# Two layers on one core: small loads, latent norms, head splits and sine tables cut up and placed elsewhere

## What is computed

```python
h = rmsnorm(x, norm_mix_g)
proj = h @ w_in                      # c_q 512, c_kv 256, k_rope, dq, dk, dv, iq, ik, iw, then gates 2 x 2048
q = rmsnorm(c_q, q_norm_g) @ w_uq    # 8 heads; latent norm over 512
ckv = rmsnorm(c_kv, kv_norm_g)       # latent norm over 256
k_nope, v = ckv @ w_uk, ckv @ w_uv
o_a = chunk_causal_attention(q, k, v)            # 8 heads of 128
o_b = attention of 8 heads over 64 keys that an index score selects
merged = sigmoid(gate_a) * (o_a @ w_branch_a) + sigmoid(gate_b) * (o_b @ w_branch_b)
x = x + merged @ w_out
x = x + peer_ffn(rmsnorm(x))         # products with two tables of 16384 x 2048, the kernel takes them densely
```

## Time and profile before

| | |
|---|---|
| median of three runs | 4248.58 us (4248.21 to 4249.74) |
| the profiled execution, its own time | 4244.8 us |
| its span, first to last instruction | 4243.2 us |
| TensorE busy | 4155.5 us, 98% |
| VectorE busy | 3134.1 us, 74% |
| ScalarE busy | 2335.8 us, 55% |
| GpSimd busy | 546.7 us, 13% |
| mean granted TensorE clock | 0.995 |

### The profile page before, as it was taken

One profiled execution on the slowest core, in us unless ns is written; L12 is line 12 of the kernel. 1 busy time (PEld: TensorE's weight loads), 2 busy tenths in 40 slices (PEclk: granted clock), 3 DMA queues, 4 the chain that ended last, 5 costly groups with the idle time before them and its releaser, 6 DMA issues.

```text
span 4243.2 us, 88247 instructions
## 1 busy us (share of the span) xinstructions
PE 4155.5 (98%) x28626; PEld 3857.7 (91%) x28626; DVE 3134.1 (74%) x5340; ACT 2335.8 (55%) x4153; POOL 546.7 (13%) x541
## 2 busy tenths in 40 slices
PE   8999999999999999999999999999999999999998
PEld 8989999999999988778889898999999998888887
DVE  6467677885999855776669978688599985555655
ACT  4445544766565545555554464467656554555554
POOL 4101010000222211111100002000022221111110
PEclk9999999999999999999999999999999999999999
DMA  6434555666666666777665544566666666667664
GB/s 245 135 100 141 182 183 187 205 205 196 192 191 190 194 211 213 231 269 228 228 207 193 175 158 150 174 206 202 199 195 190 190 194 210 218 216 237 216 218 163
DMA packets 279092, 831.29 MB, mean 196 GB/s; under 512 B 31041, under 2 KB 98369, under 8 KB 275521
## 3 DMA queue, kind: packets, MB, share of 16 engines
q1 hardware_dynamic: 274464, 812.77, 60.2%
q10 hardware_dynamic: 4512, 17.06, 1.2%
HBM read 779.37 MB, written 50.33 MB: 196 GB/s over the span
## 4 chain that ended last, share of the span: by engine, by line
PE 91%; DVE 7%; ACT 1%; issue 1%; DMA 1%; ACTq 0%; DVEq 0%; SPq 0%; POOL 0%
PE psum L1571 18%; PE psum L1573 18%; PE psum L1572 18%; PE psum L419 10%; PE psum L421 10%; PE psum L420 10%; DVE sb_w_lo L2059 2%; PE psum L402 1%; PE psum L1664 1%; DVE sb_work L1333 0%; DMA sb_raw<-in_w_proj 0%; ACT sb_w_hi L1792 0%; DVE sb_x_hl L2318 0%; PE psum L1737 0%; PE psum L381 0%
## 5 line engine op out<-in xcount | busy, mean ns | idle before, releaser
L1792 ACT CAST sb_w_hi<-sb_raw 128x512 fp32r<-128x512 f32 x2736 | 1691.3, 621 | 1736.6 <-PE psum L1573 1049.3
L2059 DVE TENSOR_TENSOR sb_w_lo<-sb_raw,sb_w_hi 128x512 fp32r<-128x512 f32 x2736 | 1879.9, 708 | 997.4 <-ACT sb_w_hi L1792 986.6
L1571 PE MATMUL psum<-sb_act_hl,sb_w_hi 128*128 128x256 f32 x6096 | 1739.2, 285 | 46.9 <-DVE sb_w_lo L2059 26.0
L1573 PE MATMUL psum<-sb_act_hl,sb_w_lo 128*128 128x256 f32 x6096 | 1727.5, 283 | 0.0
L1572 PE MATMUL psum<-sb_act_hl,sb_w_hi 128*128 128x256 f32 x6096 | 1727.3, 283 | 0.0
L1571 PEld LDWEIGHTS psum<-sb_act_hl,sb_w_hi 128*128 128x128 f32 x6096 | 1172.6, 192 | 57.7 <-issue 30.4
L1572 PEld LDWEIGHTS psum<-sb_act_hl,sb_w_hi 128*128 128x128 f32 x6096 | 1172.5, 192 | 1.1 <-issue 0.5
L1573 PEld LDWEIGHTS psum<-sb_act_hl,sb_w_lo 128*128 128x128 f32 x6096 | 1172.3, 192 | 0.0
L419 PE MATMUL psum<-sb_w_hi,sb_act_hl 128*128 128x512 f32 x2048 | 800.0, 391 | 12.0 <-DVE sb_w_lo L2059 11.8
L420 PE MATMUL psum<-sb_w_lo,sb_act_hl 128*128 128x512 f32 x2048 | 798.4, 390 | 0.0
L421 PE MATMUL psum<-sb_w_hi,sb_act_hl 128*128 128x512 f32 x2048 | 798.0, 390 | 0.0
(11 more groups left out here) (351 smaller groups left out, 3156.9 us busy)
## 6 DMA issues: line engine op xcount, KB each, us to landing
sb_raw<-in_u SPq DMA_DIRECT2D x512, 512.0 KB, 3.7
sb_raw<-in_v SPq DMA_DIRECT2D x512, 512.0 KB, 3.5
sb_raw<-in_w_z SPq DMA_DIRECT2D x82, 512.0 KB, 4.3
sb_raw<-in_w_gates SPq DMA_DIRECT2D x64, 512.0 KB, 3.5
acts_mid<-sb_acts_out SPq DMA_DIRECT2D x256, 128.0 KB, 4.3
sb_acts_in<-acts_mid SPq DMA_DIRECT2D x256, 128.0 KB, 3.3
sb_raw<-in_w_proj SPq DMA_DIRECT2D x56, 512.0 KB, 3.5
sb_raw<-in_w_q SPq DMA_DIRECT2D x48, 512.0 KB, 3.8
```

The lines of the kernel that those rows point to most:

```text
L1571: pe.matmul(ps, w_h, hi[:, k, :], start=start and kk == 0, stop=False)
L1573: mm = pe.matmul(ps, w_l, hi[:, k, :], start=False, stop=stop and kk == 3)
L1792: act.copy(w_hi[:, c, :], raw[:, 2 * par + c // 2, (c % 2) * 512:(c % 2) * 512 + 512]).then_inc(hi_ready, 1)
L2059: dve.tensor_tensor(w_lo[:, c, :], raw[:, 2 * par + c // 2, (c % 2) * 512:(c % 2) * 512 + 512], w_hi[:, c, :].bitcast(F32), ALU.subtract). ...
```

## The change

There are four parts.

1. Loads in proj1. The 3 MB of w_uq go out in four DMAs, at tiles 11, 13, 15 and 17; w_uk at 19, w_uv at 21, rotation matrices and mask at 25.
2. Latent norms in proj1. The squares and gains of both latents stand on VectorE at tile 19, TensorE's sums at 20, the first mean at 21, ScalarE's roots at 22 and 24, the reciprocal and product of c_q (and the mean of c_kv) at 23, those of c_kv at 25. The sum for c_kv has a PSUM bank of its own (3).
3. Heads. `heads_hl` takes the place and rows of `merged_hl`. `split_heads` splits four heads at each of the attention steps 24, 25 and 28, the last four behind tile 31's subtraction. branch1 reads `heads_hl`, rotated by two slots (`turned=2`), `merge` writes to `act_hl`, and out1 reads that. branch1's first `w_lo` follows in VectorE's queue at once.
4. Tables in v1. A table takes seven tiles in place of four: four small products, four small, then one large one ahead of each of three tiles; the sine and the cosine ahead of different tiles. The last ScalarE step of a table is behind tile 100 (76 before); the S5 loads go from 100 to 102, and `act_weights` from tiles 84 to 98 to tiles 103 to 110.

```diff
-SQ_BANK = [2, 2, 2, 2, 2, 7, 2, 0]
+SQ_BANK = [2, 2, 3, 2, 2, 7, 2, 0]
...
-                steps += [(48 + 4 * j, lambda j=j: sines(j)), (49 + 4 * j, lambda j=j: store(j))]
-            return steps + [(84 + 2 * n, lambda n=n: act_weights(act, n)) for n in range(8)] + [(100, lambda: act_s5_loads(act))]
+                steps += [(49 + 7 * j, lambda j=j: sines(j)), (50 + 7 * j, lambda j=j: cosines(j)), (51 + 7 * j, lambda j=j: store(j))]
+            steps += [(102, lambda: act_s5_loads(act))]
+            return steps + [(103 + n, lambda n=n: act_weights(act, n)) for n in range(8)]
...
-                link(ins)
+                    if k % 2:
+                        link(ins)
+                        yield
+                link(dve.tensor_scalar(near_t, turn_t, magic, None, ALU.add))
                 yield
-                link(dve.tensor_scalar(near_t, turn_t, magic, None, ALU.add))
                 link(dve.scalar_tensor_tensor(near_t, near_t, magic, turn_t, ALU.subtract, ALU.subtract))
+                yield
                 dve.scalar_tensor_tensor(turn_t, near_t, -1.0, near_t, ALU.mult, ALU.max).then_inc(table_in, 1)
...
-            gemm("proj1", between={9: total_of_start}, acts=split_of(1))
+            gemm("proj1", between={9: total_of_start, 20: totals_of_low_ranks}, acts=split_of(1))
             pe.wait_ge(tile_out, evac["gates1"])
             pe.wait_ge(proj_scaled, N_PROJ1)
-            sum_squares(1, low_sq[:, 0:4, :], 4)
-            sum_squares(2, low_sq[:, 4:6, :], 2)
-            pe.wait_ge(norm_ready, 1)
-            pe.wait_ge(small_loaded, 48)
+            pe.wait_ge(norm_ready, 2)
+            pe.wait_ge(small_loaded, 96)
...
-            gemm("branch1", halves=2, acts=split_of(2))
-            gemm("out1", acts=[(merged_split, 4 * c + 4) for c in range(4)], src=merged_hl)
+            gemm("branch1", halves=2, acts=split_of(2), src=heads_hl, turned=2)
+            gemm("out1", acts=[(merged_split, 4 * c + 4) for c in range(4)])
...
-            stage("proj1", plain("proj1", proj), between={10: lambda: root(0), 11: more_loads, 20: rope_sines}, begun=True)
-            root(1)
-            root(2)
+            stage("proj1", plain("proj1", proj), between={
+                10: lambda: root(0), 11: more_loads, 13: lambda: load_up(1), 15: lambda: load_up(2), 17: lambda: load_up(3),
+                19: load_keys, 20: rope_sines, 21: load_values, 22: lambda: root(1), 24: lambda: root(2), 25: load_tables}, begun=True)
...
+            stage("proj1", between={10: root_of_start, 12: angles, 14: lambda: reduce_angle(dve, link, rope_s, turns), 17: fold,
+                                    19: low_rank_squares, 21: lambda: mean_of(1, Q_RANK, EPS), 23: low_rank_queries, 25: low_rank_keys})
             dve.wait_ge(proj_scaled, N_PROJ1)
             dve.wait_ge(sin_ready, 1)
...
+            def split_heads(c):
+                dve.wait_ge(o_ready, max(8, 4 * c + 4))
+                for lo, n, slot in [(12, 2, 14), (14, 2, 0)] if c == 3 else [(4 * c, 4, 4 * c + 2)]:
+                    some, heads = heads_hl[:, slot:slot + n], o_heads[:, lo:lo + n]
+                    link(dve.tensor_copy(some[:, :, 0:T], heads))
+                    ins = dve.tensor_tensor(some[:, :, T:2 * T], heads, some[:, :, 0:T].bitcast(F32), ALU.subtract)
+                ins.then_inc(act_ready, 1)
...
+                    if step in (24, 25, 28):
+                        split_heads({24: 0, 25: 1, 28: 2}[step])
...
-            stage("gates1", steps_between=attend(), begun=False)
-            dve.wait_ge(o_ready, 16)
-            split_act(o_heads, 4 * base["branch1"], begun="branch1")
+            def last_heads(i, par):
+                if i == ATTENTION_STEPS - 1:
+                    split_heads(3)
+            stage("gates1", last_heads, steps_between=attend(), begun=False, upcoming="branch1")
```

More of the change, by code:

```diff
@@ L1105, in sines, with cosines @@
                 act.activation(made[:, 0:4, :], near_t, ACT.Sin, scale=-two_pi)
+            def cosines(j):
+                made = table_made[j % 2]
+                two_pi = 2 * math.pi * (1 - 2e-7)
                 act.activation(made[:, 4:8, :], turn_t, ACT.Sin, scale=-two_pi, bias=c_half_pi).then_inc(table_ready, 1)
@@ L1850, in more_loads, with load_up, load_keys, load_values @@
                 act.wait_ge(start_tile, 31)
[L1851 removed]
+                load_up(0)
+            def load_up(k):
+                act.dma_start(w_uq[:, k], a["w_uq"][:, k]).then_inc(small_loaded, 16)
+            def load_keys():
                 act.dma_start(w_uk, a["w_uk"]).then_inc(small_loaded, 16)
+            def load_values():
                 act.dma_start(w_uv, a["w_uv"]).then_inc(small_loaded, 16)
+            def load_tables():
                 act.dma_start(mats, a["mats"]).then_inc(consts_loaded, 16)
@@ L2017, in link @@
                 dve.wait_ge(dve_step, steps[0])
-            def rms(n, src, nt, dim, gain, dst, scr):
-                for lo in range(0, nt, 4):
-                    some = slice(lo, min(lo + 4, nt))
-                    dve.tensor_tensor(scr[:, some], src[:, some], src[:, some], ALU.mult).then_inc(sq_ready, 1)
-                dve.wait_ge(sq_ready, SQ_BASE[n] + -(-nt // 4))
-                link(dve.tensor_tensor(dst, src, gain.unsqueeze(2).broadcast_to([P, nt, T]), ALU.mult))
-                root_of(n, dim)
             def mean_of(n, dim, eps):
@@ L2040, in scaled @@
                 return dve.tensor_tensor(dst, dst, stat[:, 2, :].unsqueeze(1).broadcast_to([P, dst.shape[1], T]), ALU.mult)
-            def split_act(src, used, norm=False, begun=None):
-                if used:
-                    dve.wait_ge(quarter_used, used)
-                for c in range(4):
-                    some = slice(4 * c, 4 * c + 4)
-                    if norm:
-                        link(scaled(src[:, some]))
-                    link(dve.tensor_copy(act_hl[:, some, 0:T], src[:, some]))
-                    dve.tensor_tensor(act_hl[:, some, T:2 * T], src[:, some], act_hl[:, some, 0:T].bitcast(F32), ALU.subtract).then_inc(act_ready, 1)
-                    if begun and c == 0:
-                        low(base[begun], base[begun] % 2)
             def low(T0, par, quarters=(0, 1, 2, 3)):
@@ L2123, in root_of_start, with low_rank_squares, low_rank_queries, low_rank_keys @@
                 dve.reciprocal(start_root, stat[:, 1, :]).then_inc(root_known, 1)
-            stage("proj1", between={10: root_of_start, 12: angles, 14: lambda: reduce_angle(dve, link, rope_s, turns), 17: fold})
+            cq, ckv = proj[:, CQ:CQ + 4], proj[:, CKV:CKV + 2]
+            def low_rank_squares():
+                dve.wait_ge(proj_scaled, 6)
+                for src, at, gain in ((cq, low_sq[:, 0:4], c_qn), (ckv, low_sq[:, 4:6], c_kvn)):
+                    nt = src.shape[1]
+                    dve.tensor_tensor(at, src, src, ALU.mult).then_inc(sq_ready, 1)
+                    ins = dve.tensor_tensor(src, src, gain.unsqueeze(2).broadcast_to([P, nt, T]), ALU.mult)
+                link(ins)
+            def low_rank_queries():
+                dve.wait_ge(root_ready, 2)
+                link(dve.reciprocal(stat[:, 2, :], stat[:, 1, :]))
+                scaled(cq).then_inc(norm_ready, 1)
+                mean_of(2, KV_RANK, EPS)
+            def low_rank_keys():
+                dve.wait_ge(root_ready, 3)
+                dve.wait_ge(norm_ready, 1)
+                link(dve.reciprocal(stat[:, 2, :], stat[:, 1, :]))
+                scaled(ckv).then_inc(norm_ready, 1)
+            stage("proj1", between={10: root_of_start, 12: angles, 14: lambda: reduce_angle(dve, link, rope_s, turns), 17: fold,
+                                    19: low_rank_squares, 21: lambda: mean_of(1, Q_RANK, EPS), 23: low_rank_queries, 25: low_rank_keys})
             dve.wait_ge(proj_scaled, N_PROJ1)
             dve.wait_ge(sin_ready, 1)
-            cq, ckv = proj[:, CQ:CQ + 4], proj[:, CKV:CKV + 2]
-            rms(1, cq, 4, Q_RANK, c_qn, cq, low_sq[:, 0:4])
-            scaled(cq).then_inc(norm_ready, 1)
-            rms(2, ckv, 2, KV_RANK, c_kvn, ckv, low_sq[:, 4:6])
-            scaled(ckv).then_inc(norm_ready, 1)
             def rotated(j):
```

18 lines of the change are left out of this document (9 added, 9 removed).

## The result

| | before | after |
|---|---|---|
| median of six runs | 4247.29 us (4244.49 to 4249.74) | 4212.96 us (4210.0 to 4213.36) |
| the profiled execution | 4244.8 us | 4213.36 us |
| its span | 4243.2 us | 4211.4 us |
| mean granted TensorE clock | 0.995 | 0.996 |

The ratio is 0.9918, with a 95% interval of 0.9908 to 0.9928: 34.3 us less between the medians, 31.4 between the profiled executions. The forecast was 4223.8 with a range from 4219 to 4233. The gap is smaller between the profiled executions, where the forecast was 4220.0 and 4213.36 came, 6.6 less: the profiled one of before was near the low end of its runs, that of after is the highest of its six.

What follows compares the result with a forecast made beforehand. The prediction took TensorE, busy 98% of the span, as the bound, leaving only its idles and lowered clock to win. 3.4 + 1.8 + 1.05 - 1.0 + 6.0 + 2.55 + 5.25 + 5.7 = 24.75 gave 4223.8 us, range 4219 to 4233.

Steps and rivals of the forecast that it cites:

- What bounds the kernel: Whole kernel: TensorE is busy 98% of the span; every idle that the change aims at ends on VectorE.
- The cover of 3.6 us: Projection: a tile hides 3.6 us of VectorE step, and what is above becomes TensorE idle.
- Part 1: Projection loads: three idles gain 3.4, the idle at reduce_angle 1.8, its lowered clock 1.05 us.
- the 1.7 of lowered clock kept there: Behind reduce_angle: clock still falls after a 2.2 us idle, so 1.7 of 2.75 stays, gain 1.05 us.
- Part 2: Latent norms: idles behind the projection gain 6.0, clock there 2.55, added VectorE steps cost 1.0 us.
- Part 3: Heads, between gates1 and branch1: two idles of 3.34 and 1.91 go, gain 5.25 us.
- Part 4: Tables in v1: shorter VectorE pieces and sine and cosine apart remove idles, gain 5.7 us.
- ten idles sum to 6.5; nine give 5.7: Tables in v1: the longest idle, 0.8 us at the rates, stays; the other nine are the gain, 5.7 us.
- starving: Rival, projection: spread loads hold up the weights, 6.2 us given back, 4230 us; chance 0.09.
- thin cover: Rival: steps at 19 and 23 and head splits open idles, 6.9 us worse, 4230.7 us; chance 0.09.
- the tables lost their idles: Rival, v1, claimed the opposite: idles stay because the wait makes them, 5.7 us worse, 4229.5 us; chance 0.04.
- nothing held VectorE's queue: Rival claimed the opposite: late heads at split_heads hold VectorE's subtractions, four splits cost 30, 4254 us; chance 0.02.

Runs made afterwards that it cites:

- p1_loads: Only the spread weight loads in proj1, made in the kernel before: 4237.97 us, ratio 0.9978.
- cover: The changed kernel with one to five added, unused VectorE operations ahead of v1's tiles 12, 16, 20, 24 and 28: 4224.42 us, one execution.
- after2: The changed kernel run once more, unaltered, on the same chip as two kernels that build on it: 4211.15 us, ratio 0.9918.
- p2_norms: Only the moved latent norms, made in the kernel before, loads still in one burst at tile 11: 4238.84 us, ratio 0.9982.
- p3_heads: Only the head splits during attention, made in the kernel before: 4237.64 us, ratio 0.9979.
- p4_tables: Only the seven-tile tables in v1, made in the kernel before: 4234.75 us, ratio 0.997.
- t_together7: The kernel before with seven-tile tables, sine and cosine apart, but VectorE's table work in the two old pieces: 4241.89 us, ratio 0.9991.
- b3_all: The changed kernel with reduce_angle over three tiles, v1's rate operations over two, and the latents' squares at tiles 18 and 19: 4209.44 us, ratio 0.9913.

## Why the prediction came out as it did

**What bounds the kernel: right.** Every idle named ended on VectorE. Those at a step of VectorE's went when the step was cut or moved; the three of the load burst went when the loads were spread (`p1_loads`), so there VectorE was only the last in a row that began with late weights.

**The cover of 3.6 us: right in its own measure.** The squares' step at tile 19 lasted 121.05 to 125.16, 4.11 us, and left 0.61 of idle; `reduce_angle` lasted 90.32 to 95.59, 5.27 us, and left 1.68. They hide 3.5 and 3.6. Counted as in `cover`, from the starts (0.89 and 1.96 apart in place of 0.12) and up to what follows on VectorE (125.28 and 95.71), they hide 3.5 and 3.55. VectorE's rows in after:

```profile
90.32 1.10 DVE L2362 TENSOR_SCALAR sb_work<-sb_slots 128x768 f32<-128x768 f32 x1
...
92.05 2.95 DVE L2365 SCALAR_TENSOR_TENSOR sb_slots<-sb_work,sb_slots 128x768 f32<-128x768 f32 x3
95.03 0.56 DVE L2366 TENSOR_SCALAR sb_slots<-sb_slots 128x768 f32<-128x768 f32 x1
...
121.05 1.76 DVE L2127 TENSOR_TENSOR sb_work<-sb_work 128x1024 f32<-128x1024 f32 x1
122.74 1.21 DVE L2128 TENSOR_TENSOR sb_work<-sb_work,sb_cols 128x1024 f32<-128x1024 f32 x1
```

The first square took 1.76 and not 1.23, beside GpSimd's scaling: the half microsecond that the prediction had allowed for.

**Part 1: the idles right, their price and the clock wrong; 6.25 against 9.2.** The three idles went, and the DMA share of 0.71 is in the band of 0.6 to 0.8. Behind `reduce_angle` 1.68 was left where 2.2 was forecast, because the operations took 5.27 and not 5.8 us: in before one of the three on two inputs took 1.49 us, with a scaling of GpSimd's (99.81 to 100.53) beside it, and the others 0.96, as all three in after. The step that failed is the 1.7 of lowered clock kept there: behind that idle the clock was 1.00 in all four traces with 1.68 (after, `after2`, `p1_loads`, `cover`), and 0.50 in all six with 4.0. The prediction had weighed 2.71 against 2.43, one trace for each, and taken the dearer; over all thirteen traces the first has 0.50 behind it in each, the second in eight. No trace has an idle of 2.2 there, so what would follow the forecast's own idle is not shown. From start to start the three idles of 3.4 in all cost 4.4 (1.76, 1.52, 0.93 and, with no bracket, 0.24 apart in place of 0.12, and 0.1 more behind each), and the fourth gave 2.3 for the forecast 1.8. What is left of the 9.2 for the clock is 2.5, against 1.05.

**Part 2: right, 7.55 against 8.0.** 1.31 ahead of the up-projections (1.3 forecast), clock 1.00 there; the squares cost 0.77 and 0.07 behind them (0.9 forecast); nothing at the reciprocal (0.4 allowed, "just hidden").

**Outside the places: the idle in wq1, not foreseen.** ScalarE's timeline in `p2_norms` shows whom it waited for ahead of it, and TensorE's the idle that followed:

```profile
668.54 2.41 ACT L1793 CAST sb_w_hi<-sb_raw 128x512 fp32r<-128x512 f32 x4 [3.49 <-DMA sb_raw<-in_w_q]
```

```profile
669.94 0.39 PE L1571 MATMUL psum<-sb_x_hl,sb_w_hi 128*128 128x256 f32 x1 [1.10 <-DVE sb_w_lo L2058]
```

A load of wq1's weights came late. The same wait stands in traces without the norms moved: 2.3 us in `p3_heads`, with no idle behind it, 2.6 in `p4_tables` with 0.24, 3.1 in `p1_loads` and `t_together7` with 0.68. `t_together7` is the kernel before up to v1, where no such wait is in the trace of before; so its length differs from execution to execution. Where there is one such wait, what is above 2.4 becomes idle (3.49 and 1.10 above); after, `after2` and `b3_all` have a second of 1.3 to 1.4 behind one of 2.3, and 0.76 to 0.9 of idle. In the seven traces with the norms moved the idle was 0.76 to 1.10, in the six without 0 to 0.68. Whether the norms make it longer, and how, is open: no run here isolates it, and it is 0.4 us or so in question.

**Part 3: right, a fifth too small; 5.25 against 6.6.** The starts in that stretch of before are 3.62, 2.19, 0.44 and 0.45 us apart in place of 0.12, and 0.07 to 0.1 more behind each: 6.58, to the hundredth what the stretch gave. The two of 0.44 and 0.45 show idles of 0.17, which the prediction does not name. The wait on `o_ready` held nobody. The remark that the clock did not fall there, "so no more is to be had", read one execution as if it were all: in three of six traces it fell.

**Part 4: the mechanism right, the term mis-sized.** This is the largest error: 5.7 against 9.9 to 10.5. The step that failed is "ten idles sum to 6.5; nine give 5.7". It took TensorE's idle for TensorE's loss. Each stall cost 0.27 more than it showed (0.92 to 0.95 where it showed 0.65 to 0.68), and six of the eight tables cost a further 0.30 that has no bracket: nine times 0.27 and six times 0.30 are 4.2. It is the same error as in parts 1 and 3, and it is small where a stall is long (4.49 shown of 4.65) and large where many are short.

**The sum, again.** 24.75, and 2.9 in part 1, 0.4 in part 2, 1.3 in part 3, 4.2 in part 4: 33.6. Less 1.0 in wq1, 0.3 at the start and some 0.6 of clock elsewhere, 31.8 is the difference of the spans. Of the 8.9 that the four parts were short, some 1.4 are the clock, 0.5 the shorter `reduce_angle`, and 6.5 (1.0, 1.3 and 4.2) idle taken for loss.

**The rivals.** None came: no starving, no thin cover, the tables lost their idles, nothing held VectorE's queue. The low end of the range was built from clocks and small idles alone. It had no term for idles that count too little, though the trace of before showed matmuls of 0.39 us starting 0.227 apart.

## What to carry to other kernels

Price a stall from start to start: take the distance between the matmuls on either side, less the distance of undisturbed ones, add what the next one or two are late, and look at such distances also where no idle is shown. A step placed between tiles is free up to a sharp edge (here 2.8 to 2.9 us in v1, about 3.5 in the projection, if VectorE comes to it in time) and costs its full length above it, so cutting a step in pieces below the edge takes its whole loss away, and each piece cut below that is worth nothing more. One profiled execution shows one draw of the lowered clock; several traces of the same place say how often it falls.
